# A rearranged second half of the token mixer, and conditioning chunks that are dealt out later

## Chip, cores and metric

The kernel runs on one core of one Trainium2 chip, in one launch. The metric is the device time of the whole program in microseconds; the time before is 1420.46 us, the median of 3 runs (1420.1 to 1426.29).

## What is computed

One inference step of a trunk of two layers on 320 tokens of width 1024 (256 tokens of a new sequence, and 8 sequences with 8 new tokens each), float32. Each layer is FFN, mixer, FFN. Cut to what matters:

```python
mod = (silu(c) @ a_w + a_b).reshape(B, 3, 3, D_MODEL)       # conditioning: shift, scale, gate of 3 sublayers
modulate(y, i) = rms_norm(y, g_pre[i]) * (1 + mod[:, i, 1]) + mod[:, i, 0]
residual(y, out, i, w) = y + w * mod[:, i, 2] * rms_norm(out, g_post[i])
x = residual(x, swiglu(modulate(x, 0), f_in[0], f_out[0]), 0, 0.5)
x = residual(x, mixer(modulate(x, 1)), 1, 1.0)
x = residual(x, swiglu(modulate(x, 2), f_in[1], f_out[1]), 2, 0.5)
# mixer: z = h @ w_in, split in three groups of heads:
#   sliding-window attention with sinks and rotary (8 heads, 2 kv heads, window 128; samples read a cache)
#   HGRN2 gated recurrence in chunks of 64 (4 heads, state 64x64), then rms_norm(o) * silu(g)
#   gated short convolution of width 3
#   out = concat(o_attn, o_hg, y_conv) @ w_out; new caches and states are outputs too
```

## The kernel before, in words

Everything is stored transposed, features on partitions (8 tiles of 128) and the 320 tokens along the free axis. A product of float32 precision is made of three fp32r matmuls (`mm3`, L495 to L497): high part of the weight by high part and by low part of the activation, low part of the weight by the high part. ScalarE writes the high part of a weight tile (`hi_split`, L963), VectorE the low part (`lo_split`, L1238). Weights come through two slots `raw[0]` and `raw[1]`; SyncE (SP) issues every load in one fixed order, and `weights` makes it wait until both splits of the slot's last tile are done (`s_hi`, `s_lo`). The engines run hand-written lists of work, joined by semaphores; there is no planner.

`x` passes five gaps between sublayers, numbered n = 0 to 4 (0: first FFN to mixer; 1: mixer to second FFN; 2: end of the first layer; 3 and 4: as 0 and 1, in the second layer). In a gap (`gap`) TensorE sums the squares of the sublayer's output (`y_stats`, L551 and L553), VectorE adds the normalised output to x (`y_norm`), ScalarE squares x, TensorE sums these (`x_stats`, L545), ScalarE makes the factor (`rms`), and VectorE and ScalarE normalise and modulate x into `hmh` and `hml`, piece by piece, while TensorE begins the next product. In an FFN, 11 iterations of the first product (each ends in a SiLU on ScalarE, L1041) are followed by 4 of the second.

The conditioning matrix is the other large stream: 18 chunks of 1024 columns. Two are done at the start, the others in pairs of chunks, each pair in eight pieces of 1 MB (`piece` loads one, `partial` multiplies it, L507). When a pair is complete ScalarE copies it (`ada_copy`), TensorE transposes it (`turned`, L515), VectorE adds the bias (`mod_out`), which makes two chunks of `mod`. `HOMES` says where each piece is put: "ada" has a buffer of its own; S, B, C and P lie in tiles that are free only at certain times (B and C in the hidden values of the FFN, P in the mixer's z). `AT_GAP`, `AT_OUT` and `AT_FFN` say at which place which pieces are worked: before, pairs 2 and 3 in gap 0 and gap 1, pair 4 in the second FFN of layer 0 (one piece an iteration), pair 5 in gap 2, pair 6 in the first FFN of layer 1, pair 7 in gap 3. In gaps, five pieces go before `x_stats` and three after. `chunk_of(n, j)` is 3n + j; j = 0 is the gate of the sublayer n, j = 1 and 2 the shift and the scale of the next.

The function `mixer` on each engine is the part after the input projection. In its second half (after the scores of L755) TensorE adds the state's part to the output (L765), multiplies the samples' states (L776), transposes the samples' probabilities (L785, L786), sums squares per head (L791), makes the new states (L799), multiplies the samples' values (L807, L810), transposes the prompt's probabilities (L818, L827), does half of the first tile of the output projection, and multiplies the prompt's values (L843, L850). SP meanwhile loads the projection's weights, and in layer 0 five conditioning pieces once `mixl` is complete, then sends out states and caches; only then, in `ffn_in`, come the first tiles of the next FFN:

```python
                if l == 0:
                    sp.wait_ge(ev["mixl"], 4 * (l + 1))
                    for p in range(AT_OUT, AT_OUT + 5):
                        piece(p)
                ...
                ffn_in(l, 1, OFF_F1I)
```

Of the kernel before, what the change touches and what calls it, by code (L numbers as in the profile page):

```python
# [22 lines left out]
P = 128  # L23
# [37 lines left out]
HOMES = FIRST_HOMES + FFN_GAP + OUT_GAP + ["ada"] * 8 + FFN_GAP + ["ada"] * 8 + FFN_GAP  # L61
AT_GAP, AT_OUT, AT_FFN = {0: 16, 2: 40, 3: 56}, 24, {2: 32, 3: 48}
# [90 lines left out]
def trunk(nc, A, O):  # L153

    ctx = ExitStack()
    with ctx:
# [158 lines left out]
        for n in ("e f g b d0 e0 z0 ends eb kh0 kh itp it ktp kt gr am ds dss obk oev osq ost orr og oh "  # L315
                  "lv us un vm dsm s0n rot qk vtp vt sc scd ex exn pt ptd pv pvd ss ssd sex sexn spt sptd spv spvd "
                  "cv cst mixl kvo exd at lbd lbe gs sc0 ob sn rp ssd2 sd ebq dec").split():
            ev[n] = sem("e_" + n)
# [41 lines left out]
        def _(sp):  # L360
# [25 lines left out]
            def ffn_in(l, f, off):  # L386
# [16 lines left out]
                else:  # L403
                    both(0)
                    if n == 2:
                        sp.wait_ge(s_used[1], l * ITS + OFF_MO + IT_MO + 1)
                        for p in range(AT_OUT + 5, AT_OUT + len(OUT_GAP)):
                            piece(p)
# [28 lines left out]
            for l in range(DEPTH):  # L437
# [51 lines left out]
        def _(pe):  # L489
# [65 lines left out]
            def ffn_in(l, f, off):  # L555
# [22 lines left out]
                if n in AT_FFN:  # L578
                    done = {2: (3, 4), 3: (5, 6)}[n]
                    for it in range(IT_IN):  # L580
                        body(it, {1: done[0], 9: done[1]}.get(it), (AT_FFN[n] + it,) if it < 8 else (),
                             n if it == 0 else None)
                    return
                body(0, None, (), n)
                hold(pe)
                with pe.Fori(1, IT_IN) as it:
                    body(it)
# [27 lines left out]
            def gap(n, p):  # L615

                y_stats(n, 5)
                if p is not None:
                    for i in range(5):
                        partial(p + i)  # L620
                if n < 3 * DEPTH - 1:
                    x_stats(n + 1)
                if p is not None:
                    for i in range(5, 8):
# [24 lines left out]
            def mixer(l):  # L649
# [80 lines left out]
                pe.wait_ge(s_mod, 7 if l == 0 else 17)  # L730
# [26 lines left out]
                last.then_inc(ev["sc0"], 1)  # L757
                pe.wait_ge(ev["ebq"], l + 1)
# [10 lines left out]
                pe.wait_ge(ev["un"], 6 * (l + 1))  # L769
                hold(pe)  # L770
                for a in (0, 1):
                    for b in range(NB):
                        for e in (0, 1):
                            rows = slice(64 * e, 64 * e + 64)
                            col = a * T + TP + TS * b
                            last = mm(PS[rows, 6, a * 64 + TS * b:a * 64 + TS * (b + 1)], s0[rows, a, b, :],  # L776
                                      eb[rows, col:col + TS], start=True, stop=True)
                last.then_inc(ev["obk"], 1)
                pe.wait_ge(ev["sexn"], 2 * (l + 1))
                pe.wait_ge(ev["oev"], 2 * (l + 1))  # L780
                pe.wait_ge(ev["scd"], 2 * l + 1)
                for n in (0, 1):
                    for g in (0, 1):
                        c0 = (2 * n + g) * P
                        nc.tensor.transpose(PS[:, 6, c0:c0 + P], SS[n][:, g, 0:WIN], ident)  # L785
                        last = nc.tensor.transpose(PS[0:64, 0, c0:c0 + P], SS[n][:, g, WIN:192], ident)  # L786
                last.then_inc(ev["pt"], 1)
# [6 lines left out]
                pe.wait_ge(ev["vm"], l + 1)  # L794
                hold(pe)
                for a in (0, 1):
                    for e in (0, 1):
                        h = 2 * a + e
                        last = mm(PS[64 * e:64 * e + 64, 2 + a, :], ktok[0:64, 2, 64 * h:64 * h + 64],  # L799
                                  vm[:, h].rearrange("p b v -> p (b v)"), start=True, stop=True)  # L800
                last.then_inc(ev["dsm"], 1)

                pe.wait_ge(ev["ptd"], 4 * l + 1)
                hold(pe)
                for n in (0, 1):
# [6 lines left out]
                last.then_inc(ev["pv"], 1)  # L812

                pe.wait_ge(ev["exn"], l + 1)
                pe.wait_ge(ev["scd"], 2 * (l + 1))
                for n in (0, 1):
                    for t in range(NG):
                        last = nc.tensor.transpose(PS[:, n, t * P:(t + 1) * P], SC0[:, NG * n + t, 0:P], ident)  # L818
                last.then_inc(ev["pt"], 1)

                pe.wait_ge(ev["ssd"], 2 * (l + 1))
                pe.wait_ge(ev["s0n"], l + 1)
                pe.wait_ge(ev["orr"], l + 1)
                for s in range(4):
                    kb, n = s // 2, s % 2
                    for t in range(NG):
                        last = nc.tensor.transpose(PS[:, 2 + s, t * P:(t + 1) * P],  # L827
                                                   SC1[n][:, t // 2, t % 2, kb * P:(kb + 1) * P], ident)
                    if n:
                        last.then_inc(ev["pt"], 1)  # L830

                split_ready(0, l * ITS + OFF_MO)
                pe.wait_ge(ev["ptd"], 4 * l + 2)
                pe.wait_ge(ev["mixl"], 4 * l + 2)
# [4 lines left out]

                pe.wait_ge(ev["mixl"], 4 * l + 3)  # L840
                hold(pe)
                for n in (0, 1):
                    last = mm(PS[64 * n:64 * n + 64, 6, :], va[:, 0, 64 * n:64 * n + 64], PT0[:, n, :],  # L843
                              start=True, stop=True)
                last.then_inc(ev["pv"], 1)
                pe.wait_ge(ev["ptd"], 4 * l + 4)
                hold(pe)
                for n in (0, 1):
                    for kb in (0, 1):
                        last = mm(PS[64 * n:64 * n + 64, 2, :], va[:, kb, 64 * n:64 * n + 64], PT[:, 2 * kb + n, :],  # L850
                                  start=(kb == 0), stop=(kb == 1))
                last.then_inc(ev["pv"], 1)
# [45 lines left out]
            for l in range(DEPTH):  # L898
# [3 lines left out]
                done = 2 if l == 0 else 7  # L902
# [45 lines left out]
                gap(3 * l + 1, AT_OUT if l == 0 else None)  # L948
# [6 lines left out]
        def _(act):  # L955
# [28 lines left out]
            def x_rms(n):  # L984
# [15 lines left out]
            def x_norm(n, m, staged=None):  # L1000

                if staged is not None:
                    act.wait_ge(s_part, staged + 2)
                for i, (a, b) in enumerate(FEEDS):
# [83 lines left out]
            def mixer(l):  # L1088
# [12 lines left out]
                exps([SS[n][:, g, :] for n in (0, 1) for g in (0, 1)], 16).then_inc(ev["exd"], 1)  # L1101
                for n in (0, 1):
# [765 lines left out]
```

## Time and profile before

| what | value |
|---|---|
| median of 3 runs | 1420.46 us |
| the profiled execution | 1423.85 us |
| its span in the trace | 1422.1 us |
| mean granted clock of TensorE | 0.977 of full |
| busy: TensorE, VectorE, ScalarE, GpSimd | 1351.7, 682.1, 561.7, 76.8 us |
| read from HBM | 249.26 MB, 179 GB/s over the span |

Shares are of the whole span. TensorE is busy nearly throughout, the others less than half of the time; so their work matters where TensorE waits for it, in the gaps and in the mixer.

### The profile page before, as it was taken

Reading aid. Unit: us, or ns where it says so; the run is one execution under the profiler, and the core shown is the slowest. Engines: PE = TensorE matmul, PEld = TensorE weight load, DVE = VectorE, ACT = ScalarE, POOL = GpSimd, SP = SyncE. Lnnn points to the kernel's source line nnn. Section 1 sums busy time; section 2 is a strip of 40 time slices with the busy share of each in tenths; the row PEclk is TensorE's granted clock in tenths of the full one; section 3 lists DMA queues with packets and bytes.
Section 4 is the critical chain, followed back from the end, with each engine's and each line's share of the span. In section 5 each row is a group of like instructions: output and inputs, shape, how many; then the busy total and the mean of one; then the engine's idle time right before and its main releaser. Section 6 shows DMA issues by size and latency. Waiting matters only on the chain.

```text
span 1422.1 us, 23199 instructions
## 1 busy us (share of the span) xinstructions
PE 1351.7 (95%) x10138; PEld 1247.3 (88%) x10138; DVE 682.1 (48%) x726; ACT 561.7 (39%) x704; POOL 76.8 (5%) x97
## 2 busy tenths in 40 slices
PE   5999999999989799999999999999998889999997
PEld 3899999969868499999978999999798678999996
DVE  3434344357873544344354344443677654444433
ACT  4423333353533623334254333333534455333331
POOL 0000000000440000000000000000016000000000
PEclk8999999999989899999999999999999899999999
DMA  9875556373216565547474564556541322444440
GB/s 362 318 253 183 204 204 251 131 262 133 104 62 228 212 212 198 207 139 267 151 271 150 206 211 146 196 208 224 187 139 41 110 103 106 147 147 147 171 155 38
DMA packets 50380, 255.53 MB, mean 180 GB/s; under 512 B 7023, under 2 KB 12015, under 8 KB 30063
## 3 DMA queue, kind: packets, MB, share of 16 engines
q1 hardware_dynamic: 50110, 253.08, 49.9%
q8 instruction: 73, 1.20, 0.3%
q0 software_dynamic: 176, 1.09, 0.2%
q14 instruction: 21, 0.16, 0.0%
HBM read 249.26 MB, written 4.89 MB: 179 GB/s over the span
## 4 chain that ended last, share of the span: by engine, by line
PE 90%; ACT 3%; issue 2%; DMA 2%; SPq 2%; DVE 2%; DVEq 0%; ACTq 0%
PE PS L495 26%; PE PS L497 25%; PE PS L496 25%; PE PS L507 4%; PE PS L545 2%; DMA z<-in_ada 1%; ACT hmh L995 1%; ACT sq L995 1%; PE PS L674 1%; PE PS L693 1%; PE PS L716 1%; PE PS L878 1%; SPq L475 1%; DMA raw<-in_w_in 0%; PE PS L776 0%
## 5 line engine op out<-in xcount | busy, mean ns | idle before, releaser
L495 PE MATMUL PS<-hmh,WHI 128*128 128x320 f32 x1856 | 581.3, 313 | 19.1 <-DVE hml L1287 13.2
L496 PE MATMUL PS<-hml,WHI 128*128 128x320 f32 x1856 | 573.7, 309 | 0.0
L497 PE MATMUL PS<-hmh,WLO 128*128 128x320 f32 x1856 | 573.6, 309 | 0.0
L1238 DVE TENSOR_TENSOR WLO<-raw,WHI 128x2048 fp32r<-128x2048 f32 (+1 forms) x148 | 365.6, 2470 | 404.3 <-ACT WHI L963 404.3
L963 ACT ACTIVATE WHI<-raw 128x2048 fp32r<-128x2048 f32 (+1 forms) x148 | 303.8, 2053 | 370.7 <-PE PS L497 362.6
L495 PEld LDWEIGHTS PS<-hmh,WHI 128*128 128x128 f32 x1856 | 350.0, 189 | 52.5 <-issue 43.5
L496 PEld LDWEIGHTS PS<-hml,WHI 128*128 128x128 f32 x1856 | 350.3, 189 | 0.3
L497 PEld LDWEIGHTS PS<-hmh,WLO 128*128 128x128 f32 x1856 | 350.3, 189 | 0.0
L495 PE MATMUL PS<-hhl,WHI 128*128 128x320 f32 x704 | 216.6, 308 | 0.0
L496 PE MATMUL PS<-hhl,WHI 128*128 128x320 f32 x704 | 216.5, 308 | 0.0
L497 PE MATMUL PS<-hhl,WLO 128*128 128x320 f32 x704 | 216.5, 308 | 0.0
L496 PEld LDWEIGHTS PS<-hhl,WHI 128*128 128x128 f32 x704 | 131.9, 187 | 0.0
L495 PEld LDWEIGHTS PS<-hhl,WHI 128*128 128x128 f32 x704 | 131.9, 187 | 0.0
L497 PEld LDWEIGHTS PS<-hhl,WLO 128*128 128x128 f32 x704 | 131.9, 187 | 0.0
L1041 ACT ACTIVATE y<-PS 128x640 f32<-128x640 f32 x44 | 31.0, 705 | 184.7 <-PE PS L497 184.7
L1363 DVE TENSOR_TENSOR y<-y,PS 128x640 f32<-128x640 f32 x44 | 36.1, 821 | 125.6 <-PE PS L497 125.6
L1022 ACT ACTIVATE sq<-PS 128x640 f32<-128x640 f32 x18 | 12.7, 705 | 108.6 <-PE PS L497 108.6
L545 PE MATMUL PS<-sq,cst 128*128 128x320 f32 x96 | 32.3, 493 | 16.4 <-ACT sq L1152 11.9
L545 PEld LDWEIGHTS PS<-sq,cst 128*128 128x128 f32 x96 | 19.7, 215 | 29.9 <-issue 14.9
L1351 DVE TENSOR_TENSOR acc<-acc,sq 128x320 f32<-128x320 f32 x18 | 8.9, 495 | 72.0 <-ACT sq L1022 64.3
L1369 DVE TENSOR_TENSOR hhl<-y,hhl 128x640 fp32r<-128x640 f32 x44 | 36.0, 818 | 0.0
L1334 DVE TENSOR_TENSOR y<-y,rst 128x640 f32<-128x640 f32 (+1 forms) x30 | 20.1, 687 | 31.3 <-ACT rst L982 31.3
(235 smaller groups left out, 869.4 us busy)
## 6 DMA issues: line engine op xcount, KB each, us to landing
raw<-in_w_in SPq DMA_DIRECT2D x88, 1024.0 KB, 4.8
raw<-in_w_out SPq DMA_DIRECT2D x32, 1408.0 KB, 6.0
stage<-in_ada_w SPq DMA_DIRECT2D x66, 512.0 KB, 7.8
ada<-in_ada_w SPq DMA_DIRECT2D x62, 512.0 KB, 4.6
raw<-in_m_in SPq DMA_DIRECT2D x20, 1024.0 KB, 4.8
raw<-in_m_out SPq DMA_DIRECT2D x8, 1024.0 KB, 4.8
z<-in_ada SPq DMA_DIRECT2D x3, 1024.0 KB, 14.1
big<-in_ada SPq DMA_DIRECT2D x2, 1024.0 KB, 20.0
```

What stands on the lines that cost most here:

```text
L495: mm(out, hi, rhi, start=first, stop=False)
L496: mm(out, hi, rlo, start=False, stop=False)
L497: return mm(out, lo, rhi, start=False, stop=last)
L507: last = mm(PS[32 * j:32 * j + 32, 6 + c % 2, :], cT[:, k, :], halves[j // 2][:, (j % 2) * 512:(j % 2) * 512 + 512], start=(k == 0), stop= ...
L545: last = mm(PS[:, 5, 0:T], ones, sq[:, k, :], start=(k == 0), stop=(k == KT - 1))
L963: a_(WHI[:, slot, 0:width], raw[:, slot, 0:width], ACT.Copy).then_inc(s_hi[slot], 1)
L995: a_(out[:, k, 0:TP], sq[:, k, 0:TP], ACT.Identity, bias=mod[m][:, 8 + k, 0:1], scale=mod[m][:, 16 + k, 0:1])
L1041: a_(sg, PS[:, 0:2, 0:T], ACT.Silu).then_inc(s_gread, 1)
L1238: tt(WLO[:, slot, 0:width], raw[:, slot, 0:width], WHI[:, slot, 0:width].bitcast(F32), ALU.subtract).then_inc(s_lo[slot], 1)
L1334: done[i] = ch.mark(tt(y[:, a:b, :], y[:, a:b, :], rst2[:].unsqueeze(1).to_broadcast([P, b - a, T]), ALU.mult))
L1363: tt(hf, sg, PS[:, 2:4, 0:T], ALU.mult).then_inc(s_uread, 1)
L1369: tt(hl[:, it * 2:it * 2 + 2, :], hf, hh[:, it * 2:it * 2 + 2, :].bitcast(F32), ALU.subtract).then_inc(s_hl, 1)
```

## The change

It joins two edits. In the mixer's second half the order of the work is new on every engine: the new states come first (L799's products), then the transposes of the samples' probabilities, then the state's part of the output; the samples' probabilities and half of the prompt's first probabilities are normalised on GpSimd instead of VectorE; the probabilities of the blocks are transposed as soon as they are there, the prompt's values are multiplied ahead of the half tile of the projection, and some results lie in other PSUM banks. VectorE's low split of the projection's second tile moves to the end of its list. SP issues the next FFN's first two weight tiles among the conditioning pieces, ahead of the outputs, in both layers.

The conditioning pieces are dealt out anew: pair 4 is worked in gap 2, pair 5 in the first FFN of layer 1, pair 6 in gap 3, pair 7 in gap 4, and none in the second FFN of layer 0, which becomes a hardware loop after its first two iterations. In gap 2 and gap 4 (`WHOLE`) all eight pieces come before `x_stats`, and the pair is turned and added right after it, since the norm that follows uses it.

```diff
-HOMES = FIRST_HOMES + FFN_GAP + OUT_GAP + ["ada"] * 8 + FFN_GAP + ["ada"] * 8 + FFN_GAP
-AT_GAP, AT_OUT, AT_FFN = {0: 16, 2: 40, 3: 56}, 24, {2: 32, 3: 48}
+HOMES = FIRST_HOMES + FFN_GAP + OUT_GAP + FFN_GAP + ["ada"] * 8 + FFN_GAP + OUT_GAP
+AT_GAP, AT_OUT, AT_FFN = {0: 16, 2: 32, 3: 48}, (24, 56), {3: 40}
+WHOLE = {2: 4, 4: 7}
...
# SP, after the projection's weights
-                if l == 0:
-
-                    sp.wait_ge(ev["mixl"], 4 * (l + 1))
-                    for p in range(AT_OUT, AT_OUT + 5):
-                        piece(p)
+                first_in = l * ITS + OFF_F1I
+                sp.wait_ge(ev["mixl"], 4 * (l + 1))
+                for p in range(AT_OUT[l], AT_OUT[l] + 3):
+                    piece(p)
+                weights(first_in, 0, WIN_[(l * 2 + 1) * 2 * IT_IN], W_IN)
+                for p in range(AT_OUT[l] + 3, AT_OUT[l] + 5):
+                    piece(p)
+                weights(first_in, 1, WIN_[(l * 2 + 1) * 2 * IT_IN + 1], W_IN)
...
# TensorE, gap
+                front = 8 if n in WHOLE else 5
                 if p is not None:
-                    for i in range(5):
+                    for i in range(front):
                         partial(p + i)
                 if n < 3 * DEPTH - 1:
                     x_stats(n + 1)
+                if n in WHOLE:
+                    turned(WHOLE[n])
...
# TensorE, mixer: after the scores
+                pe.wait_ge(ev["vm"], l + 1)
+                pe.wait_ge(ev["dsr"], l + 1)
...
+                last.then_inc(ev["dsm"], 1)
+                pe.wait_ge(ev["sexn"], 2 * (l + 1))
+                pe.wait_ge(ev["un"], 6 * (l + 1))
...
+                pe.wait_ge(ev["scd"], 2 * (l + 1))
+                blocks(0, 0)
+                pe.wait_ge(ev["ptd"], 4 * l + 1)
+                pe.wait_ge(ev["oev"], 2 * (l + 1))
+                hold(pe)
+                cached(0)
+
+                pe.wait_ge(ev["osq"], l + 1)
+                for a in (0, 1):
+                    last = mm(PS[:, 4 + a, 0:T], bd, z[:, Z_I + a, :], start=True, stop=True)
+                last.then_inc(ev["ost"], 1)
+
+                cached(1).then_inc(ev["pv"], 1)
+                pe.wait_ge(ev["s0n"], l + 1)
+                blocks(1, 2)
...
+                pe.wait_ge(ev["ptd"], 4 * l + 3)
+                pe.wait_ge(ev["mixl"], 4 * l + 2)
...
# ScalarE, after the squares of x
+                if chunk is not None:
+                    ada_copy(chunk)
                 rms(5, rst[:], s_r, 1.0 / D, s_xst, n + 1)
...
# VectorE
+            def whole(n, m, layer):
+
+                mod_out(WHOLE[n])
+                dve.wait_ge(s_mod, 2 * WHOLE[n] + 3)
+                scale_ready(m, par2[:, layer, :]).then_inc(ev["sr"], 1)
...
-                lo_split(1, l * ITS + OFF_MO, W_IN)
                 dve.wait_ge(ev["dsm"], l + 1)
...
                 last.then_inc(ev["mixl"], 1)
+                lo_split(1, l * ITS + OFF_MO, W_IN)
...
# GpSimd, mixer
+                pool.wait_ge(ev["rcs"], l + 1)
+                for n in (0, 1):
+                    tt(SS[n][:, :, 0:192], SS[n][:, :, 0:192],
+                       den[:, 16 + 2 * n:18 + 2 * n].unsqueeze(2).to_broadcast([P, 2, 192]),
+                       ALU.mult).then_inc(ev["sexn"], 1)
+                pool.wait_ge(ev["rch"], l + 1)
+                tt(SC1[0][:, :, :, 0:256], SC1[0][:, :, :, 0:256],
+                   den[:, 8:12].rearrange("p (s t) -> p s t", s=2).unsqueeze(3).to_broadcast([P, 2, 2, 256]),
+                   ALU.mult).then_inc(ev["ssd"], 1)
```

## Rows read from the trace of the kernel before

**Rows 1.** The page, busy time of each engine, share of the span, instructions.
```profile
PE 1351.7 (95%) x10138; PEld 1247.3 (88%) x10138; DVE 682.1 (48%) x726; ACT 561.7 (39%) x704; POOL 76.8 (5%) x97
```

**Rows 2.** What TensorE waited for: us in total, times, longest.
```profile
PE PS L785 <- issue: 5.0, 2, 2.5
PE PS L495 <- DVE hml L1587: 3.0, 2, 1.5
PE PS L765 <- issue: 2.7, 2, 1.8
PE PS L495 <- ACT y L1137: 2.1, 2, 1.1
```

**Rows 3.** Timeline of ScalarE, two FFNs: start us, us, what [idle before, releaser].
```profile
510.33 0.70 ACT L1041 ACTIVATE y<-PS 128x640 f32<-128x640 f32 x1 [4.44 <-PE PS L497]
526.04 0.70 ACT L1041 ACTIVATE y<-PS 128x640 f32<-128x640 f32 x1 [4.44 <-PE PS L497]
541.32 0.70 ACT L1041 ACTIVATE y<-PS 128x640 f32<-128x640 f32 x1 [4.44 <-PE PS L497]
...
1241.82 0.71 ACT L1041 ACTIVATE y<-PS 128x640 f32<-128x640 f32 x1 [4.44 <-PE PS L497]
1255.90 0.71 ACT L1041 ACTIVATE y<-PS 128x640 f32<-128x640 f32 x1 [4.44 <-PE PS L497]
```

**Rows 4.** Stretches of the mixers: length, busy PE, PEld, DVE, ACT, POOL, clock, DMA, GB/s.
```profile
408.10:438.40 30.30, 23.49 (x194) 17.29 (x193) 18.69 (x30) 14.93 (x42) 2.04 (x2) 0.83 0.20 71
1105.20:1134.70 29.50, 23.50 (x194) 17.28 (x192) 17.91 (x27) 14.92 (x42) 2.04 (x2) 0.83 0.40 133
```

**Rows 5.** Timeline of the first mixer, VectorE and ScalarE.
```profile
418.34 1.23 DVE L1557 TENSOR_TENSOR split<-split,den 128x1024 f32<-128x1024 f32 x1
...
427.61 1.03 ACT L1132 ACTIVATE sq<-PS 128x1024 f32<-128x1024 f32 x1 [0.45 <-PE PS L818]
```

**Rows 6.** Timeline of GpSimd, and one VectorE row beside it.
```profile
401.69 4.04 POOL L1757 TENSOR_TENSOR big<-sq,cst 64x512 f32<-64x512 f32 x4 [0.89 <-PE PS L674]
...
457.96 0.41 POOL L1684 TENSOR_TENSOR y<-y,modB 128x128 f32<-128x128 f32 x1 [6.62 <-ACT y L1031]
465.72 2.29 DVE L1238 TENSOR_TENSOR WLO<-raw,WHI 128x2048 fp32r<-128x2048 f32 x1 [7.68 <-ACT WHI L963]
467.32 0.96 POOL L1684 TENSOR_TENSOR y<-y,modB 128x128 f32<-128x128 f32 x1 [8.95 <-ACT y L1031]
```

**Rows 7.** The gap after the first mixer: SyncE, TensorE, one stretch.
```profile
447.06 7.13 SPq L475 DMA_DIRECT2D out_vp<-big  x1
457.25 0.87 SPq L378 DMA_DIRECT2D raw<-in_w_in  x2
468.69 1.44 PE L551 MATMUL PS<-acc,cst 128*128 128x320 f32 x2 [5.40 <-DVE acc L1349]
446.00:449.00 3.00, 3.00 (x22) 3.00 (x22) 1.93 (x1) 0.00 (x0) 0.00 (x0) 1.00 1.00 380
```

**Rows 8.** The gap between the layers: TensorE, SyncE, and time to landing.
```profile
730.56 0.70 PE L551 MATMUL PS<-acc,cst 128*128 128x320 f32 x2
736.42 4.86 PE L545 MATMUL PS<-sq,cst 128*128 128x320 f32 x16
730.75 1.75 SPq L372 DMA_DIRECT2D stage<-in_ada_w  x4
DMA to landing us min/median/max: 4.7/6.3/8.1
```

**Rows 9.** The gap after the second mixer, and three first SiLUs.
```profile
1165.41 6.65 PE L545 MATMUL PS<-sq,cst 128*128 128x320 f32 x16 [4.46 <-ACT sq L988]
...
495.05 0.70 ACT L1041 ACTIVATE y<-PS 128x640 f32<-128x640 f32 x1 [1.77 <-PE PS L497]
754.86 0.70 ACT L1041 ACTIVATE y<-PS 128x640 f32<-128x640 f32 x1 [1.74 <-PE PS L497]
1185.50 0.71 ACT L1041 ACTIVATE y<-PS 128x640 f32<-128x640 f32 x1 [1.74 <-PE PS L497]
```

More of the change, by code:

```diff
@@ L403, in ffn_in @@
                 else:
-                    both(0)
-                    if n == 2:
+                    if f == 0:
+                        both(0)
+                    else:
                         sp.wait_ge(s_used[1], l * ITS + OFF_MO + IT_MO + 1)
-                        for p in range(AT_OUT + 5, AT_OUT + len(OUT_GAP)):
+                        for p in range(AT_OUT[l] + 5, AT_OUT[l] + len(OUT_GAP)):
                             piece(p)
@@ L775, in mixer, with blocks, cached @@
                             col = a * T + TP + TS * b
-                            last = mm(PS[rows, 6, a * 64 + TS * b:a * 64 + TS * (b + 1)], s0[rows, a, b, :],
+                            at = a * 64 + TS * b
+                            last = mm(PS[rows, 6, at:at + TS], s0[rows, a, b, :],
                                       eb[rows, col:col + TS], start=True, stop=True)
                 last.then_inc(ev["obk"], 1)
[L779 to L787, printed above, removed]
-                pe.wait_ge(ev["osq"], l + 1)
-                for a in (0, 1):
-                    last = mm(PS[:, 4 + a, 0:T], bd, z[:, Z_I + a, :], start=True, stop=True)
-                last.then_inc(ev["ost"], 1)
[L794 to L805, printed above, removed]
+                def blocks(n, bank):
+                    pe.wait_ge(ev["ssd"], 2 * l + n + 1)
+                    hold(pe)
+                    for kb in (0, 1):
+                        for t in range(NG):
+                            last = nc.tensor.transpose(PS[:, bank + kb, t * P:(t + 1) * P],
+                                                       SC1[n][:, t // 2, t % 2, kb * P:(kb + 1) * P], ident)
+                    last.then_inc(ev["pt"], 1)
+                def cached(n):
                     rows = slice(64 * n, 64 * n + 64)
@@ L819, in mixer @@
                 last.then_inc(ev["pt"], 1)
[L821 to L830, printed above, removed]
+                pe.wait_ge(ev["ptd"], 4 * l + 3)
@@ new lines, in mixer @@
+                pe.wait_ge(ev["mixl"], 4 * l + 2)
+                hold(pe)
+                for n in (0, 1):
+                    for kb in (0, 1):
+                        last = mm(PS[64 * n:64 * n + 64, 6, :], va[:, kb, 64 * n:64 * n + 64], PT[:, 2 * n + kb, :],
+                                  start=(kb == 0), stop=(kb == 1))
+                last.then_inc(ev["pv"], 1)
+                pe.wait_ge(ev["ptd"], 4 * l + 4)
+                hold(pe)
+                for n in (0, 1):
+                    last = mm(PS[64 * n:64 * n + 64, 7, :], va[:, 0, 64 * n:64 * n + 64], PT0[:, n, :],
+                              start=True, stop=True)
@@ L1104, in mixer @@
                     exps([SC1[n][:, t // 2, t % 2, :] for t in range(4)], 8 + 4 * n).then_inc(ev["exd"], 1)
-                act.wait_ge(ev["ex"], 3 * l + 3)
-                exps([SC0[:, h, :] for h in range(4)], 0)
+                act.wait_ge(ev["pt"], 4 * l + 1)
+                a_(PN, PS[0:64, 6, :], ACT.Copy).then_inc(ev["pnd"], 1)
+                a_(PC, PS[:, 7, :], ACT.Copy).then_inc(ev["ptd"], 1)
                 act.wait_ge(ev["ob"], l + 1)
@@ L1112, in mixer @@
                    ACT.Copy).then_inc(ev["oev"], 1)
+                act.wait_ge(ev["ex"], 3 * l + 3)
+                exps([SC0[:, h, :] for h in range(4)], 0)
                 act.wait_ge(ev["oev"], 2 * (l + 1))
@@ L1664, in _ @@
                     lo_split(1, (l + 1) * ITS, W_IN)
+                    whole(2, 2, l)
         @block.gpsimd
```

157 lines of the change are left out of this document (81 added, 76 removed).

## The prediction

> **What bounds the kernel now.** I read the page's busy lines first: TensorE is busy 1351.7 us of a span of 1422.1 [rows 1]. So the time is TensorE's work plus its pauses, and the question for every edit is whether it takes work out of TensorE's stream, fills a pause, or opens one. The list of waits [rows 2] shows four pauses in the second half of each mixer, 12.8 us in both layers together (5.0 of them at L785). Then I took the timeline at four places: an FFN with and without conditioning pieces [rows 3], the second half of the mixer [rows 4], and the gaps between sublayers [rows 7 to 9]. I call E the last matmul of a sublayer and measure a gap from E to the first SiLU of the next FFN (L1041).
>
> **1. Eight pieces leave the first layer's second FFN.** The reader is to compare start times of L1041 in [rows 3]: with a piece an iteration takes 541.32 - 526.04 = 15.28 us, with a piece and a `turned` 15.71, without either 1255.90 - 1241.82 = 14.08. A piece costs 1.20 there, a turn 0.43. Eight pieces and the turn of pair 4 leave this FFN: 8 x 1.20 + 0.43 = 10.0 us; the next FFN does one turn less: 0.4. Everything between is TensorE-bound and stays so (ACT waits 4.4 us for TensorE in each iteration, same rows). **-10.4 us.** What this has to be paid with are the pieces put elsewhere, parts 4 and 5. The two FFNs that keep or get pieces on the same pattern (gap 0, gap 3) do not change.
>
> **2. The mixer's second half, both layers.** From the last scores matmul (408.1) to the resumed output projection (438.4) pass 30.3 us, of which TensorE is busy 23.5 at a mean clock of 0.83; in the second layer it is 29.5 [rows 4]. The pauses are 2.5 at L785, 1.5 at the resumed projection (L495 waiting for L1587), 1.05 before its first half (for L1137) and 1.8 and 0.9 at L765 [rows 2]. In the new order I walk TensorE with the durations of this trace: state products 1.8 to 2.4, sample transposes 1.9, L765 1.5, L776 3.1, transposes 1.0, cached values 1.6, HGRN statistics 1.1 to 2.1, cached values 1.6, transposes 1.0 and 1.0, prompt values 1.8 and 1.0, projection 3.7. Against each I hold the other engines:
> - DVE no longer does the two sample normalisations of 384 elements, nor the first of the two 1024-element scalings of 1.23 us [rows 5]; all three go to GpSimd. GpSimd does 512 elements in about 1.01 (four in 4.04, [rows 6]), so 1.6 for the first two and 2.05 for the third, after its own work ends at 405.7: ready at 407.4 and about 410, wanted by TensorE at 410 and 416.5. Hidden; if that cover is gone they cost what they are late.
> - The recurrence (dss) is ready at 410.9, wanted at 412. The state products now stand ahead of it, which is what covers the old 1.76.
> - The sample transposes need no output evacuation any more, which is where the 2.50 stood (ACT was in its exponentials first).
> - One wait is new in place: the prompt values need the copy of PT and the low part of the sample rows; behind HGRN's Ln and Exp ACT has 1.03 + 0.6 + 1.0 [1.03: rows 5] and DVE 2.5 of arithmetic. They are late by 1 to 1.7 us. Queued behind that wait are only TensorE's own values and the projection.
> - The low split of the projection's second tile moves to the end of DVE's list: done about 432.8, wanted 3.5 us after the projection resumes. It also holds SP's reload of that buffer until 432.8; the reload is wanted at 444.7, so it is hidden.
> The walk ends at 431.8 to 432.8 instead of 438.4. All idle gone would be -6.8 plus the slow clock's share, about -8.4; a new chain through ACT could leave -3. I take **-6.0** for the first layer and, its span being shorter before, **-5.5** for the second.
> The row that could speak against moving work to GpSimd: the gate multiply L1684 takes 0.41 alone and 0.96 when it starts at 467.32 beneath a DVE subtraction of two SBUF tensors that lasts to 467.9 [rows 6]. The Trainium skill (SBUF — State Buffer, Who interferes with whom) says that a DVE instruction with two SBUF inputs and a GpSimd instruction that reads SBUF exclude each other for the whole instruction; the trace agrees (0.6 late, then 0.35 of work). By that rule the state scaling and the remaining DVE scaling (1.23) would queue behind each other and s0n would come 1.2 us later, with 1.6 us of slack by the walk; the sum would not change, and without the rule it is the same -6.0.
>
> **3. The first gap after the mixer (layer 0).** SP issues the next FFN's first tiles only at 457.25, behind five pieces and eight output transfers; ACT's squares queue behind the split of the first tile, and TensorE's L551 waits 5.40 us for them, so E is 463.29 and L1041 comes at 495.05: a gap of 31.8 [rows 7, 9]. The following gap, with the same five pieces before and three after the statistics and no such wait, takes 754.86 - 730.56 = 24.3 [rows 8, 9]. The difference is more than 5.4 since TensorE's clock was down for part of it. With the first tile issued as soon as its buffer is free (about E - 15.4) and three 1 MB pieces ahead of it at 380 GB/s (2.8 us each, [rows 7]), it lands near E - 9 and is wanted near E - 5.3. **-7.5 us** (between -5.4 and -7.5, and 0 if the tile is still late). The outputs move behind both tiles; ACT waits for them before the FFN, near E + 22, and they land by about E + 18. Covered, with little to spare. The last three pieces may land as late as E + 15 without cost, since TensorE waits for hml then anyway.
>
> **4. Gap 2 (end of layer 0): all eight pieces ahead of the x statistics.** They are needed at once, for the modulation of the very norm that follows. TensorE has E = 730.56, five pieces to 736.4, then the statistics L545 (4.86) to 741.2 [rows 8]. Three more pieces are 2.7 us, if the data are there. The last two (C0, C1) can only be issued when the FFN's last tile is used: SP issues their four halves from 730.75 to 732.5, and they land 4.7 to 8.1 us after issue [rows 8], the last near 740.2. So the eighth piece ends at 741.1 and the statistics at 745.9: +4.7 (2.7 if on time). Then transposes, two additions, one scaling and the layer's small copies stand before DVE's first normalisation, where before only Ln and Exp stood: +0.8. The three pieces taken away from behind the statistics give nothing back: TensorE waited there. **+5.5** (3.5 to 7).
>
> **5. Gap 4 (after the second mixer): eight pieces where there were none.** TensorE waits 4.46 us before L545, so with 1.5 us of y statistics E is 1159.45, and it runs L545 in 6.65 instead of 4.86 [rows 8, 9], ending at E + 12.6. L1041 comes at 1185.50, a gap of 26.05. The eight pieces are y statistics 1.35 + 7.1 + 4.8 = E + 13.3 if all data are there: only +0.6. But the last three are issued after E, and the third of them has the buffer of the first piece (P0), so it waits until that one is used, E + 2.3. 3 MB at 2.8 us each and 2 us of latency put it at about E + 11, the statistics at E + 16.7: +4.1, and the turn +0.5. **+4.6** (1 to 9: the upper end if the outputs ahead of them on SP's queue still fill it, as in layer 0, where the DMA engines were full and L475's issue took 7.13, [rows 7]).
>
> **Sum.** -10.4 - 11.5 - 7.5 + 5.5 + 4.6 = -19.3. The profiled execution took 1423.85 us (span 1422.1), so it would take 1404.5. It lies 3.4 above the median of the runs shown, 1420.46; from the median the change gives 1401.2. I predict **1401 us**.
>
> **Rivals.**
> - *Late pieces* (0.17): gaps 2 and 4 wait for DMA longer than worked out, 7 + 9 instead of 10.1, and gap 1 loses 2: -19.3 + 5.9 + 2 = -11.4, 1409. For it: SP is one queue in order, eight output transfers now stand right ahead of the pieces, and in layer 0 one output's issue was held for 7 us. Against: fewer loads are outstanding at that point now.
> - *The mixer's chain was not TensorE's* (0.10): the new order is bound by ACT and DVE behind HGRN's norm, 3 per layer: -19.3 + 5.5 = -13.8, 1407. For it: DVE is busy 18.7 and ACT 14.9 of those 30.3 us [rows 4].
> - *Everything in time* (0.10): mixer -8 per layer, gap 4 +1, gap 2 +3.5: -10.4 - 16 - 7.5 + 4.5 = -29.4, 1391.
> - *Slower* (0.05): the next FFN's first tile is now behind three pieces and behind a buffer that DVE frees 11 us later, in both layers. If it lands after it is wanted, E moves one for one in both, and everything after it on SP too. In layer 0 of before, issued at E - 6, it held E up by the 5.40 of [rows 7]. Slack is 3.5 us; each further us costs two. The change breaks even when the tile lands at about E + 5, and at E + 7 it is about 1425. Against: it would have to be issued 13 us later than its buffer is free.
> - *The pieces' relocation does nothing* (0.03): an FFN iteration stays at 15.3 because something other than the pieces sets it: -19.3 + 10.4 = -8.9, 1411.6. [Rows 3] speak against it.
>
> **Chances and range.** Main case 0.55 (1396 to 1406). With the two slower-gaining rivals and most of the faster one, 1393 to 1412 holds 8 in 10. Within 0.5% of 1420.46 is 1413.4 to 1427.6, about what a measurement of this kernel can tell from no change. Faster 0.91, same 0.06, slower 0.03; the slower rival's lighter forms fall in "same".
>
> **What would show it.** The pitch of L1041 in the first layer's second FFN should be 14.08. TensorE should take about 24 us from the last scores matmul to the resumed projection in each layer. L551 after the first mixer should have no idle before it, and that gap should be near 24.3. Gap 2 should be near 29.8 and gap 4 near 30.7, with a pause of TensorE between the pieces that ends on a DMA, and none of that where I have it on time. A first tile that ACT waits for before the squares, a long idle before the prompt values, or L1762 (state scaling) delayed past 421 would prove the respective step wrong.

## The result

The changed kernel takes 1405.12 us (median of 4 runs, 1403.69 to 1409.24); its ratio to the kernel before is 0.9878, 95% interval 0.9857 to 0.9899. A second comparison on another occasion gave 0.9903 (0.9877 to 0.9929). So the change is worth 14 to 17 us; 19.3 were forecast, and the time lies 4 us above the forecast of 1401. A fourth run of the kernel before, which took 2201.82 us, is left out of all comparisons.

The page after, with the row of TensorE's granted clock in 40 slices:

```profile
PE 1352.8 (96%) x10138; PEld 1248.3 (89%) x10138; DVE 679.0 (48%) x720; ACT 562.6 (40%) x704; POOL 85.0 (6%) x103
PEclk9999999999979999999999999999999889999999
```

TensorE is busy for 1352.8 us against 1351.7 [rows 1]: the gain is not less work but less waiting, and the pieces taken out of an FFN return as busy time elsewhere, part of it at half clock. The profiled execution is the slowest of its four (1409.24; span 1407.4, 14.7 less than before). Cut into stages by E (the last matmul of a sublayer) and by the first SiLU of each FFN (all in us):

| stage | before | after | difference | forecast |
|---|---|---|---|---|
| start to the first SiLU | 53.6 | 49.6 | -4.0 | 0 |
| first FFN | 239.5 | 239.5 | 0 | 0 |
| gap 0 to the last scores, layer 0 / 1 | 115.1 / 114.8 | 115.3 / 113.6 | -1.0 | 0 |
| second half of the mixer and projection, layer 0 | 55.2 | 51.4 | -3.8 | -6.0 |
| the same, layer 1 | 54.2 | 51.3 | -2.9 | -5.5 |
| gap 1 | 31.8 | 24.6 | -7.2 | -7.5 |
| second FFN of layer 0 | 235.5 | 225.5 | -10.0 | -10.0 |
| gap 2 | 24.3 | 28.9 | +4.6 | +5.5 |
| first FFN of layer 1 | 235.5 | 235.1 | -0.4 | -0.4 |
| gap 4 | 26.0 | 36.5 | +10.4 | +4.6 |
| last FFN and end | 236.6 | 236.2 | -0.4 | 0 |

The start is the same code in both; in the twelve traces of this study it varies between 49.6 and 53.6, so these 4.0 us are no part of the change.

The relieved FFN (ScalarE's timeline, answers to [rows 3]): one iteration is 14.08.

```profile
607.45 0.70 ACT L1064 ACTIVATE y<-PS 128x640 f32<-128x640 f32 x1 [4.44 <-PE PS L502]
621.53 0.70 ACT L1064 ACTIVATE y<-PS 128x640 f32<-128x640 f32 x1 [4.44 <-PE PS L502]
```

The second half of the mixer (answers to [rows 4]; columns as there), both layers and then stretches of 3 us of the first:

```profile
404.30:431.00 26.70, 26.32 (x194) 19.05 (x193) 17.50 (x27) 14.54 (x41) 4.48 (x3) 0.74 0.12 41
1083.30:1110.00 26.70, 26.36 (x194) 18.96 (x193) 17.49 (x27) 14.53 (x41) 4.47 (x3) 0.74 0.11 40
...
410.00:413.00 3.00, 3.00 (x45) 2.65 (x44) 1.87 (x3) 2.97 (x14) 1.86 (x2) 0.68 0.01 3
413.00:416.00 3.00, 3.00 (x19) 2.18 (x19) 1.63 (x4) 0.85 (x5) 1.17 (x1) 0.50 0.01 3
416.00:419.00 3.00, 3.00 (x6) 1.17 (x5) 1.26 (x2) 0.72 (x2) 0.00 (x0) 0.50 0.00 0
419.00:422.00 3.00, 3.00 (x22) 2.76 (x22) 2.21 (x3) 2.20 (x6) 0.00 (x0) 0.50 0.02 5
422.00:425.00 3.00, 3.00 (x15) 2.54 (x15) 0.57 (x2) 1.28 (x2) 0.00 (x0) 0.54 0.00 0
```

TensorE is busy 26.3 of 26.7 us, so the pauses of [rows 2] are gone as the walk had it, all but 0.34 us at L792. But from 411.1 to 424.7 its granted clock is 0.50: the level of 1.2 GHz instead of 2.4. These 13.6 us at the low level are more than the 10.2 us that each layer of the kernel before had (its clock is 0.50 from 411.9 to 422.1, and from 1108.2 to 1118.4). What was running, in TensorE's timeline:

```profile
407.56 1.52 PE L792 MATMUL PS<-y,raw 128*128 128x64 f32 x12 [0.34 <-issue]
409.01 2.04 PE L804 MATMUL PS<-y,s 64*64 64x8 f32 x64
410.98 1.91 PE L814 MATMUL PS<-cst,split 128*128 128x128 f32 x8
...
415.71 2.50 PE L837 MATMUL PS<-z,cst 128*128 128x320 f32 x4
```

L804 is the samples' state product (L776 before): 32 matmuls of 8 columns in the kernel's loop, each of which the trace shows as two, hence 64 in the rows, the names and the expectations. The clock falls just behind them. L837 took 2.50 for what the walk put at 1.1 to 2.1; a block of eight rows of transposes (L814) takes 1.9 instead of 1.0.

The gap after the first mixer (answers to [rows 7]): L551 is L556 now and has no idle time before it. Its start is E.

```profile
455.74 0.70 PE L556 MATMUL PS<-acc,cst 128*128 128x320 f32 x2
```

The gap between the layers (answers to [rows 8]): the eighth piece waits 1.46 us for its load, and the statistics end at E + 14.9; the forecast had 15.3.

```profile
705.81 0.70 PE L556 MATMUL PS<-acc,cst 128*128 128x320 f32 x2
715.17 1.06 PE L512 MATMUL PS<-stage,cT 128*32 128x512 f32 x8 [1.46 <-DMA stage<-in_ada_w]
716.17 4.57 PE L550 MATMUL PS<-sq,cst 128*128 128x320 f32 x16
```

The gap after the second mixer (SyncE's queue, then TensorE; answers to [rows 9]):

```profile
1135.11 1.36 SPq L483 DMA_DIRECT2D out_conv<-cso  x1
1136.58 3.09 SPq L373 DMA_DIRECT2D stage<-in_ada_w  x6
...
1134.67 0.70 PE L556 MATMUL PS<-acc,cst 128*128 128x320 f32 x2
1143.00 1.06 PE L512 MATMUL PS<-stage,cT 128*32 128x512 f32 x8 [2.41 <-DMA stage<-in_ada_w]
1145.96 1.93 PE L512 MATMUL PS<-stage,cT 128*32 128x512 f32 x8 [1.90 <-DMA stage<-in_ada_w]
1148.85 1.93 PE L512 MATMUL PS<-stage,cT 128*32 128x512 f32 x8 [0.95 <-DMA stage<-in_ada_w]
1150.71 6.78 PE L550 MATMUL PS<-sq,cst 128*128 128x320 f32 x16
```

The eight output transfers are issued up to 1136.5, then the three last pieces. They arrive at E + 8.3, 11.3 and 14.2 (E = 1134.67), TensorE waits three times, its clock falls to 0.50, the last two pieces take 1.93 each instead of 1.06 and L550 6.78 instead of the 4.57 that it took in gap 2.

### The profile page after: what moved, and what is told of

It is laid out like the page before. It is cut to its first block, busy times and chain, and to the rows that moved or that the text cites. A ratio compares the mean times of both kernels' runs of the same rounds, so it can differ in the third digit from the quotient of the medians.

```text
span 1407.4 us, 23299 instructions
## 1 busy us (share of the span) xinstructions
PE 1352.8 (96%) x10138; PEld 1248.3 (89%) x10138; DVE 679.0 (48%) x720; ACT 562.6 (40%) x704; POOL 85.0 (6%) x103
## 3 DMA queue, kind: packets, MB, share of 16 engines
q1 hardware_dynamic: 50110, 253.08, 49.6%
## 4 chain that ended last, share of the span: by engine, by line
PE 91%; ACT 3%; DMA 2%; DVE 1%; issue 1%; SPq 0%; DVEq 0%; ACTq 0%
PE PS L500 27%; PE PS L501 26%; PE PS L502 26%; PE PS L512 3%; PE PS L550 2%; ACT hmh L1016 1%; DMA stage<-in_ada_w 1%; ACT sq L1016 1%; DMA z<-in_ada 1%; PE PS L700 1%; PE PS L681 1%; PE PS L723 1%; PE PS L824 1%; PE PS L814 1%; PE PS L646 0%
## 5 line engine op out<-in xcount | busy, mean ns | idle before, releaser
L1394 DVE TENSOR_TENSOR y<-y,PS 128x640 f32<-128x640 f32 x44 | 36.1, 821 | 114.8 <-PE PS L502 114.8
L512 PE MATMUL PS<-stage,cT 128*32 128x512 f32 x320 | 40.4, 619 | 7.9 <-DMA stage<-in_ada_w 7.8
L550 PE MATMUL PS<-sq,cst 128*128 128x320 f32 x96 | 32.7, 497 | 10.7 <-ACT sq L1175 10.7
L550 PEld LDWEIGHTS PS<-sq,cst 128*128 128x128 f32 x96 | 19.8, 217 | 25.5 <-issue 15.9
L512 PEld LDWEIGHTS PS<-stage,cT 128*32 128x32 f32 x320 | 9.0, 111 | 33.2 <-issue 18.7
```

The lines of the kernel that those rows point to most:

```text
L512: last = mm(PS[32 * j:32 * j + 32, 6 + c % 2, :], cT[:, k, :], halves[j // 2][:, (j % 2) * 512:(j % 2) * 512 + 512], start=(k == 0), stop= ...
L550: last = mm(PS[:, 5, 0:T], ones, sq[:, k, :], start=(k == 0), stop=(k == KT - 1))
L1394: tt(hf, sg, PS[:, 2:4, 0:T], ALU.mult).then_inc(s_uread, 1)
```

## Experiments

Each was timed in turn with the kernel before; the gain is (1 - ratio) of the latter's median. The kernels were timed on three occasions, so they are compared by their ratios, and two of them are told apart only where their intervals are. Stages come from one profiled execution each. "Half" is the second half of the mixer, the stage above less the 24.9 us of the projection (in layer 1 of the kernel before this gives 29.3 where [rows 4] have 29.5).

| kernel | ratio (95%) | gain, us | half, layer 0 / 1 | gap 1 | gap 2 | gap 4 |
|---|---|---|---|---|---|---|
| before | | | 30.3 / 29.3 | 31.8 | 24.3 | 26.0 |
| after_again | 0.9903 (0.9877-0.9929) | 13.8 | 26.7 / 28.8 | 24.6 | 29.2 | 35.4 |
| mixer_only | 0.9939 (0.9918-0.9960) | 8.7 | 25.1 / 26.4 | 35.7 | 24.3 | 27.9 |
| dealing_only | 0.9957 (0.9937-0.9977) | 6.1 | 34.7 / 30.6 | 24.6 | 28.7 | 34.7 |
| outputs_last | 0.9859 (0.9830-0.9888) | 20.1 | 23.8 / 27.3 | 24.5 | 28.7 | 33.7 |
| own_buffer | 0.9881 (0.9855-0.9908) | 16.9 | 26.4 / 27.1 | 24.6 | 30.1 | 31.6 |
| early_two | 0.9821 (0.9797-0.9845) | 25.4 | 25.0 / 30.8 | 24.5 | 29.8 | 26.4 |
| old_dealing | 0.9868 (0.9839-0.9898) | 18.8 | 26.4 / 21.5 | 26.3 | 24.3 | 26.0 |
| fill_wide | 0.9976 (0.9958-0.9995) | 3.4 | 31.1 / 31.2 | 24.6 | 29.2 | 35.7 |
| four_not_64 | 0.9843 (0.9817-0.9870) | 22.3 | 20.3 / 19.9 | 24.6 | 28.7 | 36.4 |
| four_and_wide | 0.9871 (0.9845-0.9897) | 18.3 | 23.3 / 23.0 | 24.6 | 30.0 | 35.5 |

(early_two has two pieces inside the second projection; they are in its 30.8.)

The low clock in the halves, read from each trace in slices of 0.2 us, layer 0 / 1. "Fall" is counted from the first of the 64 narrow matmuls, which take 2.0 us in all when the clock holds; "pause" is TensorE's idle time in the half before them, nearly all of it one wait ahead of the state's part:

| kernel | pause, us | fall, us | low for, us |
|---|---|---|---|
| before | 1.8 / 1.0 | 0.6 / 0.6 | 10.2 / 10.2 |
| dealing_only (old mixer) | 1.7 / 2.5 | 1.0 / 0.1 | 20.6 / 10.2 |
| the change | 0.3 / 0.3 | 2.1 / 2.3 | 13.6 / 13.6 |
| after_again | 0.3 / 1.2 | 1.2 / 0.6 | 13.6 / 17.0 |
| mixer_only | 0.3 / 0.3 | 3.3 / 2.8 | 10.4 / 13.8 |
| outputs_last | 0.3 / 1.2 | 2.7 / 2.7 | 6.8 / 13.6 |
| own_buffer | 0.3 / 0.9 | 2.7 / 1.8 | 13.6 / 13.8 |
| early_two | 0.3 / 1.2 | 3.1 / 0.5 | 10.4 / 17.0 |
| old_dealing | 0.3 / 0.3 | 2.5 / none | 13.6 / 0 |
| fill_wide | 0.3 / 0.3 | 3.6 / 2.1 | 17.0 / 17.0 |
| four_not_64, four_and_wide | 0.3 / 0.3 | none | 0 |

**after_again**: no edit.

> The changed kernel once more, as the base of the others: 16 to 18 us faster than before (0.988). In its first trace the parts were: second FFN of layer 0 -10.0, next FFN -0.4, mixer halves -3.6 and -2.9, gap 1 -7.4, gap 2 +4.6, gap 4 +10.4. If gap 4 was an outlier of that execution (its pieces late by chance) this trace has it near 31; if it is the queue, near 36.5 again.

Gap 4 is 35.4: not an accident of one execution. The gain, 13.8, is below the 16 expected; the interval reaches 17.5.

**mixer_only** and **dealing_only**: the change in two. `mixer_only` has the hunks of the mixer on TensorE, ScalarE, VectorE and GpSimd; `dealing_only` has the new `HOMES`, `AT_*`, `WHOLE` and SP's new order.

> Only the new order of the mixer's second half (all engines); pieces and SP's order as before. Theory A (TensorE's work there runs at 1.2 GHz for half of the stretch, pauses or not): the halves take 26.7 us each instead of 30.3 and 29.5, the kernel is 6 to 7 us faster. Rival (the prediction): the halves take 24.3 and the kernel is 11 to 12 us faster, the after trace being slowed by the piece loads. The gap after the first mixer stays near 32 in both.

> The mixer as before; only the new dealing of the pieces and SP's new order (first FFN tiles ahead of the outputs). Theory A, from the after trace: -10.4 (FFNs) -7.4 (gap 1) +4.6 (gap 2) +10.4 (gap 4) = about 3 us faster. Rival (the prediction's sizes): -10.4 -7.5 +5.5 +4.6 = about 8 us faster. If the two parts do not interact, this and mixer_only add up to the whole change.

Neither theory's sizes held: 8.7 us lies between 7 and 11, 6.1 between 3 and 8, and the halves of mixer_only took 25.1 and 26.4. So the low clock in the mixer does not come from the new loads of pieces, which mixer_only doesn't have. The totals add up within the noise: 8.7 + 6.1 = 14.8 against 13.8. The gap after the first mixer did not stay near 32 in both: it is 24.6 in dealing_only, and in mixer_only it is 35.7. There the first half is 5 us shorter, but the gap behind it 3.9 longer, since SP's order is the old one:

```profile
463.05 1.43 PE L551 MATMUL PS<-acc,cst 128*128 128x320 f32 x2 [7.30 <-DVE acc L1361]
```

L551 waits 7.30 there (5.40 before, [rows 7]). In layer 0 the new order of the mixer pays 1.3 us by itself in this trace; every run with SP's new order has no such wait and gap 1 at 24.5 to 24.6 (26.3 in old_dealing). dealing_only has another surprise: its mixer is the old one, yet its halves are 34.7 and 30.6, 4.4 and 1.3 longer than before. In layer 0 the clock was low for 20.6 us instead of 10.2, and nothing here says why.

**outputs_last**, in layer 1:

```diff
                         for p in range(AT_OUT[l] + 5, AT_OUT[l] + len(OUT_GAP)):
                             piece(p)
+                        if l:
+                            late()
```

`late` is a function with the eight output transfers, which in layer 1 are taken from their place above.

> The changed kernel, but in layer 1 SP issues the eight output transfers (1.7 MB) after the last three conditioning pieces instead of ahead of them. Theory Q (gap 4 waits because the outputs stand ahead of these pieces in the full DMA queue): the last piece lands near E + 10 instead of E + 14.2, the x statistics run at full clock again, gap 4 falls from 36.5 to about 31, 5 us faster than the changed kernel. Rival R (the last piece is late because it reuses the first one's buffer and is issued only then): it still lands near E + 13 and at most 1 us is gained.

TensorE in gap 4:

```profile
1133.08 0.70 PE L563 MATMUL PS<-acc,cst 128*128 128x320 f32 x2
1142.22 1.07 PE L519 MATMUL PS<-stage,cT 128*32 128x512 f32 x8 [2.36 <-DMA stage<-in_ada_w]
1144.79 1.94 PE L519 MATMUL PS<-stage,cT 128*32 128x512 f32 x8 [1.50 <-DMA stage<-in_ada_w]
1146.65 6.45 PE L557 MATMUL PS<-sq,cst 128*128 128x320 f32 x16
```

SP issues the three pieces between E + 0.2 and 3.4 instead of 1.9 and 5.0, and the last comes at E + 11.7 instead of 14.2, between the two theories; gap 4 is 33.7, 1.7 to 2.8 us less. The x statistics took 6.45, still for the most part at the low clock, which theory Q had back at full. The kernel's ratio is 6 us better than after_again's and 3 better than that of the first comparison; both pairs of intervals overlap. Against after_again the traces show 1.7 us in gap 4 and 4.4 in the mixers' halves, whose clock was low for 20.4 us instead of 30.6.

**own_buffer**: outputs_last, and

```diff
+FFN_GAP + OUT_GAP[:7] + ["T0"]      # T0: columns 2048 to 2559 of the four split tiles
                 weights(first_in, 1, ...)
+                if l:
+                    piece(AT_OUT[l] + 7)
```

> outputs_last with one more edit: the last of the eight pieces of gap 4 gets a buffer of its own (the tails of the split tiles, free after the mixer) and is loaded before the end of the projection, so only two pieces are issued after E. Theory Q: the last piece lands near E + 9, TensorE's waits for DMA in gap 4 fall from 3.9 us to under 2, its clock stays up, and gap 4 falls from 33.7 to 29 or 30. Rival: the DMA engines are full until E + 8 whatever the order, and gap 4 stays within 1.5 us of 33.7.

```profile
1139.07 0.70 PE L572 MATMUL PS<-acc,cst 128*128 128x320 f32 x2
1148.69 1.91 PE L528 MATMUL PS<-stage,cT 128*32 128x512 f32 x8 [2.85 <-DMA stage<-in_ada_w]
1152.24 4.57 PE L566 MATMUL PS<-sq,cst 128*128 128x320 f32 x16
```

Only one wait for DMA is left, 2.85 us, more than the 2 that theory Q allowed; the last two pieces still run at the low clock (1.91 and 1.94), but L566 at the full one: 4.57. Gap 4 is 31.6, neither 29 to 30 nor within 1.5 of 33.7. The seventh piece, issued at E, still needs 9.6 us. The total is not told apart from outputs_last.

**early_two**: own_buffer, and the last three pieces in P0, P1 and T0:

```diff
+                        if l:
+                            partial(AT_OUT[l])
+                            partial(AT_OUT[l] + 1)
                         pe.wait_ge(s_sqp, 12 * l + 6)
                         pair(0, 0)
```

> own_buffer with the first two of gap 4's eight pieces multiplied in the output projection of layer 1 (between its first and second tile pair), their buffers loaded again with two of the last three pieces, so that no piece is issued after E. Theory Q: no wait for DMA is left in gap 4, it takes 26 to 27 us instead of 31.6 (36.5 in the changed kernel), the projection gets 2.0 to 2.4 us longer; together 3 us faster than own_buffer, about 1400 us. Rival: the DMA engines are full until E + 6 or later, the last pieces land no earlier than E + 8, gap 4 stays at 29 or more and the gain is under 1 us.

```profile
1137.15 0.70 PE L574 MATMUL PS<-acc,cst 128*128 128x320 f32 x2
1143.08 1.07 PE L530 MATMUL PS<-stage,cT 128*32 128x512 f32 x8 [0.86 <-DMA stage<-in_ada_w]
1144.93 4.57 PE L568 MATMUL PS<-sq,cst 128*128 128x320 f32 x16
```

No piece is issued after E, 0.86 us of waiting is left, and gap 4 takes 26.4, about as long as before with no pieces in it: theory Q. At 0.9821 this is the fastest kernel of the study, 8 to 12 us faster than the change, and its interval is clear of own_buffer's. It gained 8.5 us over own_buffer for the 3 expected; in the halves and gaps the two traces show some 3, so part of this is not accounted for.

**old_dealing**: the new mixer and SP's new order, but `HOMES`, `AT_GAP`, `AT_FFN` and what goes with them as before.

> The new mixer and SP's new order (first FFN tiles ahead of the outputs), with the conditioning pieces dealt out as in the kernel before. From the stages of the runs so far: mixer halves -3.5 each, gap 1 -7.4, everything else as before: 14 us faster than before, as fast as the whole change or up to 4 us faster, for the dealing has -10.4 in the FFNs against +4.6 and +9.4 in gaps 2 and 4. The prediction's sizes (+5.5 and +4.6) would have it slower than the whole change by 0.3 us only; if the dealing still pays, through fewer low-clock stretches, it is 3 us or more slower.

The gain is 18.8 us for the 14 expected, some 5 of it in one half that ran at full clock. 0.9868 against 0.9903 and 0.9878: the intervals overlap, so the new dealing of the pieces is not shown to gain anything, and the better estimate is on the side of the old one. As dealt in the change, 10.4 us saved in the FFNs buy 4.6 in gap 2 and 9.4 to 10.4 in gap 4. The second layer's half at full clock throughout:

```profile
1095.90:1117.50 21.60, 19.99 (x193) 14.64 (x192) 17.23 (x26) 14.20 (x41) 4.49 (x3) 1.00 0.15 50
```

That is what the new order costs TensorE when the clock holds: 21.6 us, 2.7 less than the walk.

**fill_wide**:

```diff
+                split_ready(0, l * ITS + OFF_MO)
                 pe.wait_ge(ev["pnd"], l + 1)
...
                             at = a * 64 + TS * b
+                            if e == 0 and b % 2 == 0:
+                                mm(PS[:, 6, 192:512], WHI[:, 0, 0:P], WHI[:, 0, 0:T], start=True, stop=True)
```

> The changed kernel with eight matmuls of 320 columns (results thrown away) set between the 64 matmuls of 8 columns in the second half of the mixer: 1.2 us more work per layer. Theory N (the clock falls because TensorE, though busy, runs narrow matmuls there): the fall that begins 6 to 9 us into the second half in every run so far comes later or not at all, and the half takes 23 to 25 us instead of 26.7. Rival F (the fall has another cause, as the mixture before it, or eight are too few): the clock falls at the same place and the half takes 1 us longer.

```profile
403.90:435.00 31.10, 30.76 (x199) 21.68 (x200) 17.22 (x26) 14.63 (x41) 4.41 (x3) 0.73 0.10 35
```

(The fall "6 to 9 us into the second half in every run so far" holds for the new order; with the old one it came after 3 to 4 us.) `split_ready` makes TensorE wait for the first weight tile of the projection, which the wide matmuls read; the trace shows no pause there. The eight cost more than the 1.2 us put down for them:

```profile
408.42 0.39 PE L806 MATMUL PS<-WHI 128*128 128x320 f32 x1
408.74 0.40 PE L807 MATMUL PS<-y,s 64*64 64x8 f32 x8
409.08 0.42 PE L806 MATMUL PS<-WHI 128*128 128x320 f32 x1
```

A group of one wide and eight narrow takes 0.67 us at full clock, where eight narrow took 0.25 (2.04 for 64), so the stretch is 3.4 us longer. Theory N failed in this form: the half takes 31.1 us, 4.4 more, the clock falls while this stretch runs, and it is low for 17.0 us in both layers. The kernel gains only 3.4 us.

**four_not_64**:

```diff
-                    for b in range(NB):
-                        for e in (0, 1):
...
+                    for e in (0, 1):
+                        last = mm(PS[rows, 6, a * 64:a * 64 + 64], s0[rows, a, 0, :],
+                                  eb[rows, col:col + 64], start=True, stop=True)
```

> The changed kernel with the samples' state product done by 4 matmuls of 64 columns instead of 64 of 8 (all with the first sequence's state; this part of the result is left out). It takes about 1.8 us of work away per layer. Theory N: the clock does not fall, or falls several us later, and the half takes 19 to 21 us instead of 26.7, the kernel is 10 us or more faster than the changed one. Rival F: only the 1.8 us per layer go, the low stretch of 9 to 12 us stays.

```profile
406.90:427.20 20.30, 18.39 (x135) 12.91 (x136) 16.67 (x26) 14.10 (x41) 4.45 (x3) 1.00 0.16 54
```

The clock is 1.00 in both layers. The half falls from 26.7 to 20.3 and 19.9, 6.4 us and more, though the stretch itself became only 1.6 us shorter (0.38 for 1.97). The whole kernel gained less than the 10 us over the change that theory N had: 22.3 against 13.8 and 17.3. Its interval is clear of after_again's, but not of the first comparison's.

**four_and_wide**: four_not_64 with `for i in range(3): mm(PS[:, 6, 192:512], WHI[:, 0, 0:P], WHI[:, 0, 0:T], ...)` before each of the four, and `split_ready` as in fill_wide.

> four_not_64 (four matmuls of 64 columns for the samples' state product, the same part of the result left out) with twelve matmuls of 320 columns beside them, so that this stretch of TensorE takes as long again as the 64 narrow ones (1.8 us). Theory N (narrow matmuls bring the clock down): it stays at 1.00, and the second half takes about 22 us, 1.8 more than in four_not_64. Rival L (what counts is the length of the stretch of float32 work, or chance): the clock falls to 0.50 as in the changed kernel and the half takes 26 to 29 us.

```profile
406.70:430.00 23.30, 21.33 (x146) 15.04 (x147) 17.12 (x26) 14.30 (x41) 4.44 (x3) 1.00 0.13 47
```

The stretch with the wide matmuls, from its first row to the row behind it:

```profile
411.26 0.68 PE L804 MATMUL PS<-WHI 128*128 128x320 f32 x3
...
414.80 1.09 PE L815 MATMUL PS<-cst,split 128*128 128x128 f32 x8
```

It takes 3.5 us, longer than the 2.0 of the 64 narrow matmuls (so the half is 3 us longer than in four_not_64, not 1.8), and the clock stays at 1.00 in both layers: theory N, not L.

What this shows, and what not. Take the halves with the new order and a pause of only 0.3 us: with the 64 narrow matmuls the clock fell in 11 of 12, without them in none of 4. That is the evidence that in the new order they bring it down, and fill_wide adds that putting wide ones between doesn't help. Whether it is their 8 columns or their number (each with a load of its stationary operand) was not separated; four_not_64 changes both. In the other halves something else has a part. TensorE's wait ahead of the state's part came back, with 0.9 to 1.2 us, in layer 1 of four traces of the new order (after_again, outputs_last, own_buffer, early_two), and in two of these the clock fell when only 0.5 to 0.6 us of the narrow matmuls had run. With the old mixer the pause was 1.0 to 2.5 us and the clock fell after 0.1 to 1.0; in layer 1 of dealing_only that is at the first of them:

```profile
1092.90:1096.80 3.90, 1.43 (x12) 1.42 (x12) 3.76 (x9) 0.00 (x0) 0.00 (x0) 1.00 0.73 256
1096.80:1107.00 10.20, 8.13 (x79) 6.41 (x80) 7.67 (x11) 8.03 (x30) 2.04 (x2) 0.50 0.02 6
```

So there the pauses stay a likely cause, and no run of the old order without the narrow matmuls was made. Why one half of old_dealing was spared stays open as well.

## Why the prediction was right, and where it was not

The direction, and what each edit trades, were right; the time lies in the range, and at the edge of the main case of 1396 to 1406. That it is so near owes something to luck: two terms together missed by 10.6 us, and the second comparison (13.8 us) would put it at 1407. By its steps:

1. **FFN.** -10.4 forecast, -10.4 measured; pitch 14.08.
2. **Mixer.** Half of the mechanism held: the pauses at L765, L785 and before the projection are gone but for 0.3 us, GpSimd's work is hidden, the low split on time (it ends at 431.0). The size was off, -6.7 in the profiled run for -11.5, and the step that failed is the clock. The walk put "the slow clock's share" among what goes with the pauses and priced the statistics, transposes and values mostly at the full clock; instead the low stretch grew from 10.2 to 13.6 us, with TensorE busy all through it. With the clock up the walk would have been too careful instead (21.6 for its 24.3), but with the 64 narrow matmuls in place only that one half was. For the new order four_not_64 and four_and_wide show them as the cause. They stood in the kernel before too (3.15 us at L776, for 2.04 at full clock), where the clock of 0.83 [rows 4] may come from them, from the pauses or from both.

The rule weighed there shows more than it did before:

```profile
403.86 1.89 POOL L1803 TENSOR_TENSOR split<-split,den 128x1024 f32<-128x1024 f32 x1 [0.34 <-DVE den L1558]
404.87 2.59 DVE L1564 SCALAR_TENSOR_TENSOR raw<-raw,dec 128x128 f32<-128x128 f32 x6
...
411.14 3.03 POOL L1808 TENSOR_TENSOR s<-s,dec 128x512 f32<-128x512 f32 x2 [5.39 <-PE PS L804]
411.50 1.76 DVE L1587 TENSOR_TENSOR split<-split,den 128x1024 f32<-128x1024 f32 x1
```

The recurrence L1564 takes 2.59 (six instructions) and starts beside GpSimd's scaling L1803, before it took 1.92 alone; the state scaling L1808 takes 3.03 for 2.04 and VectorE's L1587 1.76 for 1.23 [rows 5]. That is the exclusion of the Trainium skill (SBUF — State Buffer, Who interferes with whom), and the trace agrees: the state scaling ends about 1 us late, for the 1.2 worked out. No wait of TensorE in the profiled run comes from it: the new state is complete at 415.9 and wanted at 421.0.

3. **Gap 1.** -7.2 for -7.5. That SP's order is the cause is shown by dealing_only, which has the new one with the old mixer and a gap of 24.6, and by mixer_only, which has the old order of SP and a gap of 35.7.
4. **Gap 2.** +4.6 for +5.5: the last piece's wait was 1.46 us, for the 2 foreseen, and the turn cost less.
5. **Gap 4.** +10.4 for +4.6, the term that failed. The last piece came at E + 14.2, not E + 11: 3.2 us. The forecast had the outputs' issue in its upper bound only; outputs_last gives 2.5 of it back. The rest is the clock, which I had counted as staying up: behind the last landing the last piece took 0.9 too long and L550 1.9 (6.78 for 4.86), although the same statistics had shown 6.65 in this gap before [rows 9]. The upper bound of this term (+9) was too low.

The rival *late pieces* is thus what happened in gap 4 and not in gap 2. The rival *the mixer's chain was not TensorE's* was near in size (5.5 us less in the mixer, measured 4.8) for the wrong reason: TensorE was busy nearly all the time. The slower rival did not occur; the first tile was never waited for. The profiled execution as a whole is only 4.6 us off (-14.7 for -19.3), less than the 10.6 of terms 2 and 5, mostly because its start was 4.0 us shorter by chance.

## What to carry to other kernels

A busy engine isn't an engine at speed: before pricing a reordered stretch, look at the granted clock in it and find out by an edit which instructions bring it down, for removing the pauses may not bring it back. When transfers are moved into a gap, write down for each when its buffer is free and what stands ahead of it in the queue; here eight outputs issued first cost the last piece 2.5 us, and in early_two, with no piece issued after E and two worked ahead of it, the gap was 9 to 10 us shorter. Two edits that end in the same wait (a shorter mixer, an earlier first tile) are also worth trying together: most of what the shorter mixer gained in layer 0 was lost again in the wait behind it.

## What the runs showed of the hardware

In the mixer's second half in its new order, with a pause of only 0.3 us ahead of them, 64 fp32 matmuls of 8 columns (2 us, TensorE busy throughout) went with a granted clock of 0.50 in 11 of 12 halves. It fell 1.2 to 3.6 us after the first of them and stayed low for 6.8 to 17.0 us, while TensorE was nearly always busy. Four matmuls of 64 columns in their place (8 rows in the trace), with or without wide ones beside them, left it at 1.00 in 4 of 4. Eight wide matmuls put between the narrow ones made the low stretch no shorter (17.0 us). This also makes the time of one kernel vary: halves of the same mixer code took 21.5 to 28.8 us.
